# Attention scores on half the array rows: each head from its own 64 partitions into its own PSUM bank, with queries scaled beforehand

## The reference

```python
DILATED_PATTERNS = ((128, 1), (512, 4), (2048, 16))     # window, dilation
...
    s = jnp.einsum('nrbqhc,nrbkhc->nrbhqk', qs, kb) * ATTN_SCALE      # blocks of 128 queries
    s = jnp.where(ok[None, None, :, None], s, NEG_INF)                # band of 128, own and previous block
    lse = jax.nn.logsumexp(s, axis=-1)
    pr = jnp.exp(s - lse[..., None])
    o = jnp.einsum('nrbhqk,nrbkhc->nrbqhc', pr, vb)
...
    w = jax.nn.softmax(lse, axis=0)                                   # combine the three patterns
    return jnp.einsum('pnlh,pnlhc->nlhc', w, o)
```

## Time and profile before

| | |
|---|---|
| median of 3 runs | 3014.56 us (3014.53 to 3019.99) |
| profiled execution, span from first to last instruction | 3016.2 us |
| mean granted TensorE clock | 0.969 |
| PE busy | 2880.6 us (96%) |
| DVE / ACT / POOL busy | 1738.7 / 1482.5 / 850.4 us |
| attention stage, about | 592 to 1144 us of the span |

### The profile page before, as it was taken

One profiled execution on the slowest core, in us unless ns is written; L12 is line 12 of the kernel. 1 busy time (PEld: TensorE's weight loads), 2 busy tenths in 40 slices (PEclk: granted clock), 3 DMA queues, 4 the chain that ended last, 5 costly groups with the idle time before them and its releaser, 6 DMA issues.

```text
span 3016.2 us, 44469 instructions
## 1 busy us (share of the span) xinstructions
PE 2880.6 (96%) x15264; PEld 2717.8 (90%) x15264; DVE 1738.7 (58%) x2949; ACT 1482.5 (49%) x2648; POOL 850.4 (28%) x960
## 2 busy tenths in 40 slices
PE   7898899999999998999999999999999999999998
PEld 6898898867666897999999999999999999999998
DVE  7867767689622675555546555455554555545543
ACT  5565655666655783554334443344433443344431
POOL 4566665545200244111321112111221112211111
PEclk8999999989899998999999999999999999999999
DMA  5344343455444333434434344343533444334332
GB/s 163 98 155 138 109 148 123 139 199 187 156 140 142 102 120 127 119 114 144 131 118 136 113 149 126 113 142 112 155 122 108 145 132 139 114 113 144 114 119 75
DMA packets 151107, 395.26 MB, mean 131 GB/s; under 512 B 19605, under 2 KB 66581, under 8 KB 146821
## 3 DMA queue, kind: packets, MB, share of 16 engines
q1 hardware_dynamic: 114480, 349.69, 37.0%
q10 hardware_dynamic: 34196, 34.58, 3.7%
q0 software_dynamic: 2240, 8.52, 0.7%
HBM read 358.17 MB, written 34.57 MB: 130 GB/s over the span
## 4 chain that ended last, share of the span: by engine, by line
PE 83%; DVE 5%; issue 5%; POOL 2%; ACT 2%; DMA 0%; DVEq 0%; POOLq 0%; ACTq 0%; SPq 0%
PE bank L1523 22%; PE bank L1525 22%; PE bank L1524 22%; PE bank L1594 7%; PE bank L1619 2%; PE bank L1606 2%; PE bank L1682 2%; PE bank L1618 1%; DVE xc L934 1%; DVE pm L1010 0%; DVE d L959 0%; PE bank L1678 0%; PE bank L1679 0%; DVE h_lo L870 0%; POOL sq L1288 0%
## 5 line engine op out<-in xcount | busy, mean ns | idle before, releaser
L857 DVE TENSOR_TENSOR w_lo<-stage,w_hi 128x1024 fp32r<-128x1024 f32 x500 | 652.3, 1305 | 348.0 <-ACT w_hi L471 340.3
L1523 PE MATMUL bank<-hb_hi,w_hi 128*128 128x416 f32 x2240 | 792.4, 354 | 21.4 <-DVE hb_lo L1163 20.2
L471 ACT ACTIVATE w_hi<-stage 128x1024 fp32r<-128x1024 f32 x500 | 527.7, 1055 | 548.8 <-PE bank L1525 529.9
L1525 PE MATMUL bank<-hb_hi,w_lo 128*128 128x416 f32 x2240 | 794.0, 354 | 0.0
L1524 PE MATMUL bank<-hb_lo,w_hi 128*128 128x416 f32 x2240 | 786.1, 351 | 0.0
L1523 PEld LDWEIGHTS bank<-hb_hi,w_hi 128*128 128x128 f32 x2240 | 423.4, 189 | 30.3 <-issue 16.9
L1524 PEld LDWEIGHTS bank<-hb_lo,w_hi 128*128 128x128 f32 x2240 | 424.0, 189 | 7.6 <-issue 0.6
L1525 PEld LDWEIGHTS bank<-hb_hi,w_lo 128*128 128x128 f32 x2240 | 422.9, 189 | 3.0
L1523 PE MATMUL bank<-ff_hi,w_hi 128*128 128x416 f32 x960 | 338.0, 352 | 0.0
L1525 PE MATMUL bank<-ff_hi,w_lo 128*128 128x416 f32 x960 | 337.3, 351 | 0.0
L1524 PE MATMUL bank<-ff_lo,w_hi 128*128 128x416 f32 x960 | 335.4, 349 | 0.0
(11 more groups left out here) (246 smaller groups left out, 4275.0 us busy)
## 6 DMA issues: line engine op xcount, KB each, us to landing
stage<-in_w SPq DMA_DIRECT2D x500, 512.0 KB, 3.6
past<-in_past SPq DMA_DIRECT2D x32, 1152.0 KB, 6.1
vb<-out_v SPq DMA_DIRECT2D x48, 256.0 KB, 2.8
attention_rows<-ob SPq DMA_DIRECT2D x32, 264.0 KB, 2.1
oc<-attention_rows SPq DMA_DIRECT2D x16, 528.0 KB, 3.9
xs<-in_x ACTq DMA_DIRECT2D x40, 208.0 KB, 2.5
qb<-query_rows SPq DMA_DIRECT2D x16, 512.0 KB, 7.8
xT<-in_x ACTq DMA_DIRECT2D x4, 1664.0 KB, 10.1
```

The source lines that it names most:

```text
L471: e.activation(w_hi[s][:], stage[s % STAGE][:], ACT.Copy).then_inc(hi_ready, 1)
L857: e.tensor_tensor(w_lo[s][:], stage[s % STAGE][:], w_hi[s][:].bitcast(F32), ALU.subtract).then_inc(lo_ready, 1)
L1523: e.matmul(out, w_hi[s][:, k], hi, start=start, stop=False)
L1525: return e.matmul(out, w_lo[s][:, k], hi, start=False, stop=stop)
```

## The change

- The matmul of a head uses only that head's 64 partitions of `qT` and `kT`, straight from these tiles. `qp`, its zeroing on POOL and `copy_q` on ACT go.
- The two heads of a unit write to two banks, `bank[2*(t%2)]` and `bank[2*(t%2)+1]`; two units share the four banks, so the scores of unit u wait for the maxima of unit u-2, where they waited for unit u-4.
- Queries leave PSUM in the first stage multiplied by -1/8 (`ACT.Identity` with a scale, for all query and key tiles). Maximum becomes minimum, the mask is +1e30, and the minimum itself is the bias of the exponential, with scale -1. The DVE instruction `nm` goes.
- The 48 blocks are written out, with constant addresses.
- The first scores wait for all rotary work; SP's `load_y(0)` waits for the last scores, where it waited for the last query copy.

```diff
-        qp = [sb(f"qp{i}", [P, JT, 2, P], on=in_p) for i in range(2)]
...
-        def attention(e, body):
-            def turn(order, k, then):
-                for n in range(4):
-                    body(blk(order, k, n), blk(order, k, n + 1) if n < 3 else then)
-            for order in range(3):
-                turn(order, 0, blk(order, 1, 0))
-                with e.Fori(1, 3) as k:
-                    turn(order, k, blk(order, k + 1, 0))
-                turn(order, 3, blk(order + 1, 0, 0) if order < 2 else None)
+        BLOCKS = [blk(order, k, n) for order in range(3) for k in range(4) for n in range(4)]
+        def attention(body):
+            for cur, nxt in zip(BLOCKS, BLOCKS[1:] + [None]):
+                body(cur, nxt)
+        def strided(start, n, step):
+            return slice(start, start + (n - 1) * step + 1, step)
+        def score_bank(t, hd):
+            return bank[2 * (t % 2) + hd]
...
-            e.wait_ge(q_copied, 48)
+            e.wait_ge(qk_done, 4 * 48)
             e.wait_ge(smp_stored, 16)
             load_y(0)
...
-            def copy_q(b):
-                for hd in range(2):
-                    rows = slice(HD * hd, HD * hd + HD)
-                    ins = e.activation(qp[b.n % 2][rows, :, hd, :], qT[rows, :, bass.ds(b.first, P, b.dil)], ACT.Copy)
-                ins.then_inc(q_copied, 1)
...
-                        e.activation(raw[i][:], b[:, 0:C], ACT.Copy).then_inc(evacuated[t % 4], 1)
+                        e.activation(raw[i][:], b[:, 0:C], ACT.Identity, scale=-SCALE if 2 * j + i < JT else 1.0).then_inc(evacuated[t % 4], 1)
...
-                    ins = e.activation(v, v, ACT.Exp, bias=nm[:, t, hd:hd + 1], scale=SCALE,
+                    ins = e.activation(v, v, ACT.Exp, bias=st[:, b.n, 0, 2 * t + hd:2 * t + hd + 1], scale=-1.0,
...
-                    ins = e.tensor_tensor_reduce(pm[t][:, hd, k0:], bank[t][:, 2 * P * hd + k0:2 * P * (hd + 1)], band[:, k0:],
-                                                 1.0, NEG, ALU.add, ALU.max, st[:, b.n, 0, 2 * t + hd:2 * t + hd + 1])
-                ins.then_inc(maxed, 1)
-                e.wait_ge(maxed, u + 1)
-                e.tensor_scalar(nm[:, t], st[:, b.n, 0, 2 * t:2 * t + 2], -SCALE, None, ALU.mult).then_inc(masked, 1)
+                    ins = e.tensor_tensor_reduce(pm[t][:, hd, k0:], score_bank(t, hd)[:, k0:2 * P], band[:, k0:],
+                                                 1.0, POS, ALU.add, ALU.min, st[:, b.n, 0, 2 * t + hd:2 * t + hd + 1])
+                ins.then_inc(masked, 1)
...
             def scores(b, t):
                 u = 4 * b.idx + t
-                if t == 0:
-                    e.wait_ge(q_copied, b.idx + 1)
-                if not (isinstance(u, int) and u < 4):
-                    e.wait_ge(masked, u - 3)
+                if u == 0:
+                    e.wait_ge(roped, 8 * CHUNKS)
+                if u >= 2:
+                    e.wait_ge(masked, u - 1)
                 n = 2 * P if b.prev else P
-                keys = bass.ds(b.first - P * b.dil if b.prev else b.first, n, b.dil)
+                queries = strided(b.first, P, b.dil)
+                keys = strided(b.first - P * b.dil if b.prev else b.first, n, b.dil)
                 for hd in range(2):
-                    last = e.matmul(bank[t][:, 2 * P * (hd + 1) - n:2 * P * (hd + 1)], qp[b.n % 2][:, t, hd], kT[:, t, keys],
-                                    start=True, stop=True)
+                    rows = slice(HD * hd, HD * hd + HD)
+                    last = e.matmul(score_bank(t, hd)[:, 2 * P - n:2 * P], qT[rows, t, queries], kT[rows, t, keys], start=True, stop=True)
                 last.then_inc(qk_done, 1)
```

More of the change, by code:

```diff
@@ L51 @@
 SCALE = HD ** -0.5
-NEG = -1e30
+POS = 1e30
 PAST_KEYS = 9
@@ L642, in y_out @@
                 e.wait_ge(y_turned, y + 1)
-                if not (isinstance(y, int) and y < 2):
+                if y >= 2:
                     e.wait_ge(yt_stored[par], 8 * (y - par))
@@ L717, in _ @@
             turned(blk(0, 0, 0), 0)
-            attention(e, body)
+            attention(body)
             def ahead_c(n, t):
@@ L1106, in spread_out @@
                     e.wait_ge(spread_zeroed, 2)
-                if not (isinstance(seq, int) and seq < 2):
+                if seq >= 2:
                     e.wait_ge(past_used, b.idx - 2)
@@ L1117, in body @@
                 par = cur.n % 2
-                again = cur.order == 2 and not (isinstance(y, int) and y < 1)
+                again = cur.order == 2 and y >= 1
                 for t in range(4):
@@ L1126, in body @@
                         spread_out(cur)
-                    if cur.order == 0 and not (isinstance(cur.idx, int) and cur.idx == 0):
+                    if cur.order == 0 and cur.idx > 0:
                         sample_keys(cur, t)
@@ L1136, in body @@
                 e.wait_ge(pv_done, 4 * cur.idx + 4)
-                if cur.order < 2 or isinstance(y, int) and y < 2:
+                if cur.order < 2 or y < 2:
                     e.wait_ge(os_stored[par], 16 * (2 * cur.turn + cur.n // 2))
@@ L1319, in chunk @@
                         square_sum(c + 1, range(KD)[4 * j:4 * j + 4])
-                    if not more and j == 2:
-                        e.wait_ge(hl_ready, KD * CHUNKS)
-                        for i in range(2):
-                            e.memset(qp[i][:], 0.0).then_inc(qp_zeroed, 1)
                     for i in range(2):
@@ L1393, in combine @@
                 e.wait_ge(cm_max, 2 * y + 2)
-                if not (isinstance(y, int) and y == 0):
+                if y > 0:
                     e.wait_ge(cm_dve, 3 * y)
@@ L1422, in body @@
                     e.wait_ge(qb_loaded[cur.n % 2], 8 * (cur.idx - cur.n % 2) + 16)
-                    if not (isinstance(cur.idx, int) and cur.idx == 0):
+                    if cur.idx > 0:
                         e.wait_ge(past_used, cur.idx)
@@ L1426, in body @@
                     e.tensor_tensor(dst[1], dst[1], qb[cur.n % 2][:], ALU.mult).then_inc(sk_prod, 1)
-                if cur.order == 2 and not (isinstance(y, int) and y < 1):
+                if cur.order == 2 and y >= 1:
                     combine(y - 1, (cur.n - 1) % 4)
@@ L1600, in turn @@
                 e.wait_ge(exp_done, u + 1)
-                if not (isinstance(u, int) and u < 2):
+                if u >= 2:
                     e.wait_ge(pt_ready, u - 1)
@@ L1623, in turn_y @@
                 e.wait_ge(cm_dve, 3 * y + 3)
-                if not (isinstance(y, int) and y < 1):
+                if y >= 1:
                     e.wait_ge(yt_ready, y)
@@ L1706, in body @@
                     values(cur, t)
-                    if cur.order == 2 and not (isinstance(y, int) and y < 2) and t == 0:
+                    if cur.order == 2 and y >= 2 and t == 0:
                         turn_y(y - 2, cur.n % 2)
@@ L1831, in sample_masks @@
     past = np.zeros((P, 3 * P), np.float32)
-    past[:, :P] = np.where(np.arange(P)[None] >= tok[:, None], 0.0, NEG)
-    new = np.full((P, 2, 3, SMP), NEG, np.float32)
+    past[:, :P] = np.where(np.arange(P)[None] >= tok[:, None], 0.0, POS)
+    new = np.full((P, 2, 3, SMP), POS, np.float32)
     key = np.arange(SMP)
```

106 lines of the change are left out of this document (42 added, 64 removed).

## The result

The changed kernel took 3056.02 us (median of 4 runs, 3054.89 to 3057.0), the kernel before 3014.66 beside it: a ratio of 1.013 (95% interval 1.0116 to 1.0145), some 41 us slower where 32 us faster were forecast. The profiled spans are 3055.3 and 3016.2 us.

A forecast was written before the change was run, and what follows sets the result against it. PE was taken to bound the kernel, mainly through the score matmuls. The terms -43 + 23 - 4 - 3 - 5 = -32 us on the median 3014.6 gave 2983 us, range 2924 to 3026.

The forecast's parts named there:

- What bounds the kernel: Whole kernel: PE, busy 96% of the span, sets the pace; the change pays through the score matmuls or hardly at all.
- Overlap of the heads: Score matmuls: head 0's second pair runs beside head 1's first, three pair times a unit, -43 us; partial overlap 0.50.
- the rival of full overlap: Score matmuls: both heads run side by side throughout and a unit halves, -107 us, total about 2919 us; chance 0.13.
- Changes of shape: Between scores and transposes or values: two changes in each of 192 units at 0.06 us, +23 us (0 to 46).
- Query loads with gaps: Orders 0 and 1: weights loaded from `qT` with gaps of 4 or 16 elements, taken at nothing, upper end 14 us.
- Bias product and written-out blocks: Bias product leaving DVE, -4 us in order 0 and -3 in order 1; blocks written out in order 1, -5 us.
- The clock: Rival, orders 0 and 1: more PE waits slow blocks by 1.65 us; some 20 cancel the gain, all 32 give 3036; chance 0.09.
- What would show it: Score groups about 1.4 us in order 0, 0.72 in orders 1 and 2; blocks near 11.4 and 9.0 in orders 0 and 2.
- two signs of being wrong: Prediction wrong if half-row matmuls run one by one, or if PE begins to wait for DVE or ACT.

The follow-up runs named there:

- e6: Changed kernel, but both heads of a pair read partitions 0 to 63, so their score matmuls cannot run beside each other: 3306.94 us.
- e2: e1 with one edit: each score matmul reads only its own head's 64 partitions of the padded query copy and the keys: 3033.58 us.
- e1: Changed kernel with scores reading all 128 partitions again, from zero-padded query copies made by ACT: 3003.81 us, ratio to before 0.9951.
- e7: Changed kernel plus 18 constant matmuls over all 128 partitions ahead of the fifth and of the ninth block of order 0: 3033.14 us.
- e10: Changed kernel plus one stretch of 18 constant matmuls over partitions 0 to 63, ahead of the fifth block of order 0: 3069.35 us.
- e12: Changed kernel with full-row scores from padded query copies in orders 0 and 1, plus a long wait ahead of block 8 of order 0: 3001.77 us.
- e17: e9 with a second output bank for blocks 3, 5, 7 and 9, so blocks 4 to 10 skip the wait for DVE's copy: 2975.79 us, ratio 0.9867.
- e3: Changed kernel plus one constant matmul over all 128 partitions before each unit's scores in orders 0 and 1: 3099.33 us.
- e15: e9 with full rows also in the first block of each turn of order 0 (blocks 4 and 8): median 2996.0 us, ratio 0.9918.
- e5: Changed kernel, but order 0's scores read queries and keys of adjacent columns instead of every fourth: 2990.1 us.
- e8: Changed kernel with full-row scores from padded query copies in order 0, and 64-row scores with queries from the copies in order 1: 2996.76 us, ratio 0.9923.
- e18: Changed kernel with full-row scores from padded query copies in orders 0 and 1, plus the second output bank of e17: 2994.04 us, ratio 0.9929.
- e9: Changed kernel with full-row scores from padded copies in order 1 and blocks 0, 1, 2, 12, 13 of order 0: 2992.9 to 2997.6 and 3013.5 to 3020.6 us.
- e13: The kernel of e9 executed a second time, unchanged: 2997.53 us.
- e16: The kernel of e9 executed a third time, unchanged: 2991.9 us.

## Why the prediction was wrong

**What bounds the kernel** was right: PE, and nothing else, decided the time.

**Overlap of the heads**: the mechanism was another one, and that the size came out near is luck. The prediction let the second pair of head 0 run beside the first of head 1, three pair times to a unit. In the trace the two heads start together. Two narrow windows of PE's timeline, 1061.10 to 1061.30 and 1061.55 to 1061.65, show the matmuls under way in the unit of order 2: two from 1061.04, two more from 1061.36.
```profile
1061.04 0.49 PE L1562 MATMUL bank<-kT,qT 64*128 64x256 f32 x2
...
1061.36 0.38 PE L1562 MATMUL bank<-kT,qT 64*128 64x256 f32 x2
```
That is the rival of full overlap, which had 0.13. It agrees with the Trainium skill ("TensorE: Matmul & The Clock Gate", Measured speedup vs the span model), by which such matmuls follow each other by some 4 ns: here under 0.01 us lies between the two. Still no unit halves: 1.21, 0.73 and 0.64 us stand against 0.91, 0.445 and 0.46. Of 107 us, 48 x (1.82 - 1.21) + 64 x (0.89 - 0.73) + 60 x (0.92 - 0.64) = 56 were saved, and some 2 in the narrow units of order 0, where 43 were taken.

**Changes of shape**: too cheap, and over the upper end. Outside the scores, a block of order 2 fell from 9.18 to 8.68 us, while its scores gave 4 x 0.28 = 1.12; the missing 0.62 over eight changes is 0.078 each, an estimate of 30 us for all 384. Inside them lies what the overlap fell short by, 49 us. e6, where nothing runs side by side, shows where: a unit of order 2 at 1.00 starts its matmuls at 1145.09, 1145.41, 1145.63 and 1145.85 and the transposes at 1146.15. The middle ones are 0.22 us apart, about as before (0.23); next to the changes of shape it is 0.32 and 0.30. So the loss sits at the changes, in order 2 at least. The rule on draining at a switch ("TensorEngine Tiling (Array Packing)" of the Trainium skill, Key Properties) agrees. With some 41 of the 49 inside the scores, an estimate again, the term is near 70 us, where 23 were taken and 46 were the upper end.

**Query loads with gaps**: taken at nothing, wrong in order 1. Scores there take 0.73 us, and 0.61 in e2 with contiguous queries: 64 x 0.12 = 8 us, inside the range of 0 to 14. They are the other 8 of the 49. The other 13 of the 20.5 us between the two kernels' order 1 go with the clock, 0.81 against 0.89.

**Bias product and written-out blocks**: -12 forecast, -15 measured by e1.

With these terms alone the change would be worth -58 + 30 - 15 = -43 us, the 8 of the gaps being inside the -58. The clock took that and 41 more, some 84 us.

**The clock** is the step that failed. The prediction priced it as some 20 isolated blocks at 1.65 us each that new waits of PE would slow, and gave it 0.09. Two things were wrong in it. It looked for new waits, when the waits that take the clock down were there before (order 0 stood at 0.95, not at 1.00); what the change took away is what brought the clock back, the full-row scores (e1 against e2, e7 against e10, e12). So not single blocks but all 16 of order 0 ran at 0.50, from 598 us on. And the price came from order 1, whose blocks are made of other work. In order 0 a turn takes 57.9 us in the changed kernel (17.06 + 16.12 + 14.51 + 10.21) and 38.0 in e17 (9.21 + 9.07 + 10.49 + 9.18): 5.0 us a block, three times 1.65. The stretch from 950 to 962.5 at 1.00 held sample values that read all 128 partitions; it was no argument about 64.

**What would show it** named the block times and the waits, and no clock. Blocks of order 0 near 11.4 us were expected and took 10.2 to 17.1, which shows that something was wrong, not what; the page's clock line does. Of its two signs of being wrong neither came: the heads did not run one by one, and PE's share of busy time did not fall.

Open: what TensorE misses in 64-row work can't be seen in a trace. Nor does every result go by the rows: the full-row matmuls of e3 and the full-row block 8 of e15 did not bring the clock back, and the 64-row blocks of e5 did. Nor is it shown why a wait of 0.17 us costs the clock at one border and not at another, and why 64 rows in order 1 took 183.8 us in e2 and 190.4 in e8.

## What to carry to other kernels

A shorter instruction mix can be a slower one: ask of each edit on TensorE not only what it costs but whether the clock comes back afterwards, and look for the places where it falls today. Packing heads into row halves paid where PE never waits (order 2, -9 us) and, once a wait of 0.17 us was removed, in order 0 too (e17 against e18, -18 us); next to waits it cost 41 us (e2 against e1, order 0). Keep a form of the work that regains the clock behind each long wait, look in the trace whether it does (the full rows of blocks 12 and 13 did in e9, those of block 8 in e15 did not), and use the short form in between.

## What the runs showed of the hardware

- PE at 96% busy says nothing of its clock: order 0 was 96% busy at 0.50 (changed kernel) and 98% at 0.98 (e1). The Trainium skill ("TensorE: Matmul & The Clock Gate", What's actually happening) ties the clock to how busy the engine has been. The falls behind waits agree with it (e7, 4.09 us); the profile's busy share does not show it, and between e1 and e2 the rows of the array made the difference.
- Spaced scores take the same time at both levels: 1.21 us a unit at 0.50 (changed kernel) and at 1.00 (e17), while transposes and values go from 1.42 to 2.65.
- Behind a wait of 0.17 us the 64-row blocks stayed at the lower level for 61 us (e13, e16) and 123 us (e9). The Trainium skill ("TensorE: Matmul & The Clock Gate", A second HAM failure mode: psum-queue depth-cycling) tells of short idles between groups of matmuls that make the clock go back and forth; in e9, e13 and e16 it went down and did not come back until full rows had run.
- Matmuls of two heads on different halves of the rows start within 0.01 us of each other (1061.04), but a group of them between matmuls on all rows takes 0.64 us where half of the old group is 0.46.
